# Entry of a one-core decoder trunk: norm weights loaded in two parts, x transposed ahead of the first products

## The reference

```
for l in range(DEPTH):
    xn = rms_norm(x, norm_mix_g[l])
    proj = xn @ w_in[l]                  # q, k, v and the inputs of three other mixers
    q = rope(q, positions); k = rope(k, positions)
    merged = sum of four mixers, each projected and gated by sigmoid(xn @ w_gate[l] + b_gate[l])
    x = x + merged @ w_o[l]
    hn = rms_norm(x, norm_ffn_g[l])
    gu = hn @ w_ffn_in[l]
    x = x + (silu(gu[..., :FF_DIM]) * gu[..., FF_DIM:]) @ w_ffn_out[l]
return rms_norm(x, final_norm_g)
```

## Time and profile before

| | before |
|---|---|
| device time, median of 3 runs | 831.18 us (830.91 to 831.44) |
| the profiled execution: its own time | 831.92 us |
| the profiled execution: its span | 830.2 us |
| TensorE busy | 817.8 us (99%) |
| VectorE busy | 612.2 us (74%) |
| ScalarE busy | 459.0 us (55%) |
| GpSimd busy | 153.6 us (18%) |
| DMA | 156.17 MB, mean 188 GB/s |
| mean granted TensorE clock | 0.994 of full speed |

### The profile page before, as it was taken

How to read it: one execution, slowest core, us unless ns; L and a number is a source line. 1 busy time by engine, 2 the same in 40 slices (tenths; PEclk the granted TensorE clock), 3 DMA queues, 4 the chain that set the end, 5 groups by cost and what they waited for, 6 DMA issues and landing times.

```text
span 830.2 us, 12730 instructions
## 1 busy us (share of the span) xinstructions
PE 817.8 (99%) x4963; PEld 721.3 (87%) x4963; DVE 612.2 (74%) x732; ACT 459.0 (55%) x625; POOL 153.6 (18%) x147
## 2 busy tenths in 40 slices
PE   7999999999999999999999999999999999999997
PEld 6999888888989999999999988888899888888885
DVE  3989788986786666656697798888687667666664
ACT  4847776634465545454565567765355545454544
POOL 6005756064000000000000285623300000000000
PEclk8999999999999999999999999999999999999999
DMA  9876555556545755564558655464645464655451
GB/s 277 274 217 197 196 165 178 185 196 219 188 139 163 238 183 174 199 205 161 195 170 254 199 179 165 167 231 159 204 157 198 152 199 159 221 181 192 162 178 51
DMA packets 103533, 156.17 MB, mean 188 GB/s; under 512 B 4016, under 2 KB 68834, under 8 KB 103488
## 3 DMA queue, kind: packets, MB, share of 16 engines
q1 hardware_dynamic: 100928, 152.45, 55.6%
q0 software_dynamic: 1328, 1.79, 0.7%
q10 hardware_dynamic: 1232, 1.31, 0.5%
HBM read 152.39 MB, written 1.05 MB: 185 GB/s over the span
## 4 chain that ended last, share of the span: by engine, by line
PE 93%; DVE 3%; ACT 1%; DMA 1%; issue 1%; POOL 0%; DVEq 0%; ACTq 0%; POOLq 0%
PE bank L1047 19%; PE bank L1049 10%; PE bank L992 8%; PE bank L994 8%; PE bank L993 8%; PE bank L935 7%; PE bank L936 7%; PE bank L937 7%; PE bank L1024 5%; PE bank L1023 5%; PE bank L1022 5%; DVE w_lo L1386 1%; DMA gain_rows<-in_norm_ffn_g 1%; ACT w_hi L625 1%; PE bank L1128 1%
## 5 line engine op out<-in xcount | busy, mean ns | idle before, releaser
L1386 DVE TENSOR_TENSOR w_lo<-raw,w_hi 128x2048 fp32r<-128x2048 f32 x136 | 320.7, 2360 | 133.7 <-ACT w_hi L625 133.1
L625 ACT ACTIVATE w_hi<-raw 128x2048 fp32r<-128x2048 f32 (+1 forms) x144 | 263.9, 1839 | 131.4 <-PE bank L994 55.8
L1047 PE MATMUL bank<-act,w_hi 128*128 128x512 f32 x704 | 247.6, 395 | 0.0
L1049 PE MATMUL bank<-act,w_lo 128*128 128x256 f32 x704 | 196.9, 280 | 0.0
L1047 PEld LDWEIGHTS bank<-act,w_hi 128*128 128x128 f32 x704 | 132.0, 188 | 30.3
L1049 PEld LDWEIGHTS bank<-act,w_lo 128*128 128x128 f32 x704 | 132.8, 189 | 0.4
L992 PE MATMUL bank<-w_hi,act 128*128 128x512 f32 x288 | 114.3, 397 | 0.0
L994 PE MATMUL bank<-w_hi,act 128*128 128x512 f32 x288 | 112.3, 390 | 0.0
L993 PE MATMUL bank<-w_lo,act 128*128 128x512 f32 x288 | 112.1, 389 | 0.0
L625 ACT ACTIVATE qk<-bank 128x256 f32<-128x256 f32 (+1 forms) x96 | 37.5, 394 | 76.4 <-PE bank L1049 76.3
L935 PE MATMUL bank<-act,w_hi 128*128 128x256 f32 x256 | 74.0, 289 | 0.4 <-DVE act L1409 0.2
(11 more groups left out here) (243 smaller groups left out, 1417.3 us busy)
## 6 DMA issues: line engine op xcount, KB each, us to landing
raw<-in_w_ffn_in SPq DMA_DIRECT2D x44, 1024.0 KB, 5.1
raw<-in_w_gate SPq DMA_DIRECT2D x32, 1024.0 KB, 5.5
raw<-in_w_ffn_out SPq DMA_DIRECT2D x22, 1024.0 KB, 4.9
raw<-in_w_in SPq DMA_DIRECT2D x20, 1024.0 KB, 5.8
raw<-in_w_o SPq DMA_DIRECT2D x8, 1024.0 KB, 5.0
raw<-in_w_proj_b SPq DMA_DIRECT2D x4, 1024.0 KB, 4.9
gates<-qk SPq DMA_DIRECT2D x32, 64.0 KB, 4.4
raw<-in_w_proj_a SPq DMA_DIRECT2D x2, 1024.0 KB, 4.9
```

What stands on the lines that cost most here:

```text
L625: return nc.scalar.activation(o, i, ACT.Copy)
L1047: nc.tensor.matmul(bank[b + f], hi[:, k, fs], act2[:, k, :, :].rearrange("p h s -> p (h s)"), start=(k == 0), stop=False, skip_group_check ...
L1049: last = nc.tensor.matmul(main(b)[:, f, :], lo[:, k, fs], act_hi[:, k, :], start=False, stop=(k == KT - 1), skip_group_check=True)
L1386: V.tensor_tensor(w_lo[slot][:, :], raw[slot][:, :], w_hi[slot][:, :].bitcast(F32), ALU.subtract)\
```

## The change

The norm weights of the mixers (`norm_mix_g`, 16 rows) are loaded by ACT's queue right behind x piece 0, and those of the feed-forward part (`norm_ffn_g`) by POOL's queue behind the parameter rows and `icnt`. They are turned and copied separately: the first at the entry, the second at unit 4 of layer 0 beside the parameter rows. ACT's queue now carries x piece 0, the weights, x piece 2, quarter 1; SP's carries quarter 3 as well, ahead of unit 1. PE runs 34 dummy products instead of 24, turns x piece 0 before the norm weights, then pieces 1 and 2, and runs 12 dummies; piece 3 is turned after quarter 0. On DVE `reduce_angles` moves from unit 1 to unit 2, behind `norm_scale`.

```diff
@@ sp
             load_x(sp, 3)
+            load_quarter(sp, 0, 3)
             for i in range(4):
                 load_quarter(sp, 1, i)
@@ gpsimd
             nc.gpsimd.memset(zeros[:, :], 0.0).then_inc(pre_const, 1)
-            for i, name in enumerate(("norm_mix_g", "norm_ffn_g")):
-                pool.dma_start(gain_rows[i * L * KT:(i + 1) * L * KT, :], T[name].rearrange("l (r p) -> (l r) p", p=P))\
-                    .then_inc(gain_in, 16)
             nc.gpsimd.memset(ident[:, :], 0.0).then_inc(pre_const, 1)
...
             pool.dma_start(icnt[:, :, :], inv_count).then_inc(icnt_in, 16)
+            pool.dma_start(gain_rows[FFN_GAINS:FFN_GAINS + L * KT, :], T["norm_ffn_g"].rearrange("l (r p) -> (l r) p", p=P))\
+                .then_inc(ffn_gain_in, 16)
@@ scalar
             load_x(act, 0)
+            act.dma_start(gain_rows[0:L * KT, :], T["norm_mix_g"].rearrange("l (r p) -> (l r) p", p=P))\
+                .then_inc(gain_in, 16)
+            load_x(act, 2)
             load_quarter(act, 0, 1)
-            load_x(act, 2)
-            load_quarter(act, 0, 3)
...
+                    if l == 0:
+                        copy(gains[:, L * KT:2 * L * KT], bank[6][:, P:P + L * KT])
                     copy(par[:, 0:r0], bank[6][:, 0:r0])
@@ tensor, at unit 4
+                    if l == 0:
+                        pe.wait_ge(ffn_gain_in, 16)
+                        fg = slice(FFN_GAINS, FFN_GAINS + L * KT)
+                        nc.tensor.transpose(bank[6][:, P:P + L * KT], gain_rows[fg, :], ident[fg, fg])
                     nc.tensor.transpose(bank[6][:, 0:N_ROWS], rows[:, :], ident[0:N_ROWS, 0:N_ROWS])\
@@ tensor, entry
             pe.wait_ge(pre_const, 1)
-            warm(24)
+            warm(34)
             pe.wait_ge(pre_const, 3)
-            pe.wait_ge(gain_in, 16 * 2)
-            nc.tensor.transpose(bank[0][:, 0:2 * L * KT], gain_rows[:, :], ident[0:2 * L * KT, 0:2 * L * KT])\
+            first_x(0)
+            pe.wait_ge(gain_in, 16)
+            nc.tensor.transpose(bank[0][:, 0:L * KT], gain_rows[0:L * KT, :], ident[0:L * KT, 0:L * KT])\
                 .then_inc(pre_pe, 1)
-            first_x(0)
-            warm(4)
             first_x(1)
-            warm(8)
+            first_x(2)
+            warm(12)
             pe.wait_ge(gains_ready, 1)
             for i in range(4):
-                if i in (1, 2):
-                    first_x(i + 1)
+                if i == 1:
+                    first_x(3)
                 pe.wait_ge(act_lo_ready, i + 1)
                 last = quarter(0, i)
@@ vector
             dve.wait_ge(pre_pe, 1)
-            V.tensor_copy(gains[:, :], bank[0][:, 0:2 * L * KT]).then_inc(gains_ready, 1)
+            V.tensor_copy(gains[:, 0:L * KT], bank[0][:, 0:L * KT]).then_inc(gains_ready, 1)
...
-                    if l == 0 and u == 1:
-                        reduce_angles()
                     if u == 1 + (l == 0):
                         norm_scale(l, 0)
+                    if l == 0 and u == 2:
+                        reduce_angles()
                     misc(l, u)
```

More of the change, by code:

```diff
@@ L114 @@
 N_ROWS = 70
+FFN_GAINS = 32
 DVE_CHAIN_PER_LAYER = 66
@@ L197, in build @@
         rows = sb("rows", [N_ROWS, P])
-        gain_rows = sb("gain_rows", [2 * L * KT, P])
+        gain_rows = sb("gain_rows", [FFN_GAINS + L * KT, P])
         gains = sb("gains", [P, 2 * L * KT])
@@ L309, in build @@
         gain_in = sem("gain_in")
+        ffn_gain_in = sem("ffn_gain_in")
         gains_ready = sem("gains_ready")
```

## The result

| | before | after |
|---|---|---|
| device time, median | 831.20 us (830.31 to 831.65, 20 runs) | 832.58 us (832.04 to 834.39, 20 runs) |
| ratio after / before | | 1.0019, interval 1.0012 to 1.0026 |
| the profiled execution: its own time, its span | 831.92, 830.2 us | 832.36, 830.6 us |
| first product of unit 0 | 12.04 | 8.78 |
| first product of unit 2 | 26.20 | 25.27 |

What follows compares the result with a forecast made beforehand. Two chains, from the norm weights through TensorE and from unit 2's landing, were taken to bound unit 2's start. Terms -0.9 (unit 2), -0.45 (norm), +0.1 (transpose) sum to -1.25, giving a median of 829.9 us, range 828.5 to 831.7.

Steps and rivals of the forecast that it cites:

- two chains that meet at unit 2: At unit 2's first product: one chain through TensorE from the norm weights, one from unit 2's landing, meeting at 26.20.
- landing 21.0: Unit 2's load: still lands at 21.0, with the same 5.36 MB ahead of its end; range 20.2 to 21.6.
- first product of unit 2 at 25.3: Unit 2: products start at 25.3 instead of 26.2, 0.9 us gained, as DVE starts the low part earlier.
- TensorE through unit 1 at 21.2: Units 0 and 1: TensorE is through at 21.2, or by about 24 if the clock is low at first.
- no wait left in front of the norm's product: Norm's product after unit 3: the 0.45 us wait goes, as DVE has the norm ready at about 34.7.
- the sum against the profiled execution: Whole kernel: -0.9 - 0.45 + 0.1 = -1.25, so 830.67 us for the profiled execution's own time.
- The clock: Rival at the wait before unit 2: the clock falls, costing 1.4 to 2.8 us, total 831.3 to 832.7; chance 0.15.
- The base of the sum: Whole kernel: the runs' median stands 0.74 us below the profiled time, at 831.18, so it becomes 829.9.
- The transpose: At unit 4: one more transpose on TensorE for the feed-forward weights, taken as 0.1 us, up to 0.28.
- The uneven engines: Unit 2's landing: some DMA engines ahead of others; rival of a landing at 20.2 gives 829.1 us, chance 0.22.
- it doesn't do what it says: Entry: norm weights land at 7.75 or beyond; time stays the forecast's, loss only beyond about 10; no separate chance.
- the whole entry gain: Rival at unit 2: it does not bind, needing a landing at 17; -5.0 - 0.45 + 0.1 gives 825.8 us; chance 0.04.

Runs made afterwards that it cites:

- after_again: The changed kernel run again unchanged as a control: 832.83 us, ratio 1.0017 to the kernel before; its profiled execution took 830.63 us.
- fill_wait: The changed kernel with 64 more dummy products between unit 1 and unit 2: 831.19 us, ratio 0.9995 to the kernel before.
- no_dummies: The changed kernel without its 34 and 12 dummy products: 831.42 us, ratio 0.9999 to the kernel before.
- before_filled: The kernel before with 90 dummies at its start instead of 24: 831.55 us, ratio 1.0006.
- late_spread: Changed kernel with POOL's loads held until unit 2 lands, matrices until unit 5 lands, one transpose at unit 4, dummies spread (40, 8, 8): 826.39 us.
- before_pool_late: The kernel before with POOL's loads behind the norm weights held until unit 2 has landed: 830.87 us, ratio 1.0000.

## Why the prediction was wrong

**What held.** The view of two chains that meet at unit 2, and each time on it: landing 21.0 (measured 20.88), first product of unit 2 at 25.3 (25.27), TensorE through unit 1 at 21.2 (21.1), a wait of 4.1 us (4.00), and no wait left in front of the norm's product. The 21.2 came true partly by luck. I had unit 0 start between 9.3 and 10.8 and its last quarter held to about 14 by ACT and DVE. It started at 8.78, below that range, and from 10.97 on the products follow each other without a wait; the last quarter began at 13.91 by TensorE's own pace. The execution of after_again without a fall took 830.63, and the sum against the profiled execution had said 830.67. That agreement is luck in part too: its unit 2 began 0.3 us earlier than forecast (24.98), and its transposes cost 0.2 us more.

**The clock (the step that failed).** The forecast put the fall of the clock in the new wait at nothing. I had the mechanism as a rival, with the right place and a price of 1.4 to 2.8 us, and gave it 0.15. The measured 832.58 lies inside that rival's 831.3 to 832.7. The range up to 831.7 took in only the lowest 0.4 of those 1.4 us, not the lower half as I wrote. In the two profiled executions the other terms came close: -0.93 for -0.9, -0.44 for -0.45, +0.31 for +0.1; the clock's +1.56 stands where the sum has no term. It is the normal case: one timing of 11 in after_again, and none of the 20 of after, lies below 831.9, and the fall in the others is inferred from that. The measured price is 1.5 us in the pair of traces and 1.6 between the medians of after_again and fill_wait. I had argued that the wait was about as long as the idle time after which the clock fell in the earlier trace rows, called that open, and then priced it as unlikely. A wait about as long as one that goes with a fall in a trace at hand speaks for it. no_dummies shows that even 2.3 us can do.

**The base of the sum.** I took the gain at unit 2, 0.9 us, from one profiled execution (26.20), and then moved the whole result down by the 0.74 us by which that execution lay above the median. I read these as the same 0.7 us. In the profiled execution TensorE came late to unit 2 after the low clock of the earlier trace rows; before_filled shows that without that loss the kernel before is held by the landing as well. If all behind unit 2's start is alike, the median of 831.2 belongs to a start at some 25.5 (26.20 less 0.7) and not at 26.2, and the change has little to gain there. It is an inference for the runs without a trace, and what held unit 2 in them is not shown. The numbers nearly close with no gain there at all: 831.2 - 0.44 (norm) + 0.31 (transpose) = 831.07 without a fall, and fill_wait measures 831.19; with 1.6 for the fall 832.7, and after measures 832.58.

**The transpose.** I took 0.1 for it from a gap of 0.03, with 0.28 as the upper end; it measured 0.31. One small transpose between products had cost next to nothing; a second one beside it did.

**The uneven engines.** I counted it as a chance for a gain. The landing varied between 20.2 and 21.6 in the traces with POOL's loads in place, so the range of 20.2 to 21.6 held, but it moves before and after alike and favours neither.

**Rival "it doesn't do what it says"** did not come: the norm weights were turned at 6.15.

**Rival "the whole entry gain"** did not come either, but I had written that nothing brings unit 2 in by 17. Holding POOL's loads does (17.88, and 16.14 to 16.54 in three other traces), and late_spread's 826.39 is near that rival's 825.8.

## What to carry to other kernels

Before an entry is made faster, follow the first transfer that it does not touch from its landing through every split to the products: if that chain ends where TensorE arrives now, an earlier arrival only becomes a wait, and a wait of a few us may cost TensorE's clock on top. Such a gain comes out once the other chain is shortened too, here by holding 1 MB of loads, of which TensorE reads the first at 45 us (3.6 us under the kernel before), or by cutting the unit into quarters (3.0 us). The hold brings nothing without the early entry; the quarters were not tried without it. A profiled execution that lies above the median must be asked what in it was slow before its waits are put down as a gain; the same loss must not be counted as a gain and as an offset. And a granted clock of 1.00 is checked against the rate of the rows before it is believed.

## What the runs showed of the hardware

At unit 2 the clock fell about 1 us after TensorE had begun to work again, not during the wait: in after the wait ended at 25.27 and the fall came at 26.3; in no_dummies it ended at 24.59 and the clock was 0.78 of full speed from 25 to 26 on average and 0.50 from 26 on. At the entry of before it fell during the wait, near 7.6. The length of the wait alone doesn't decide it: 2.31 us brought a fall, 2.92 us in after_again did not. The granted clock can also read 1.00 where TensorE works at half rate: in before_pool_late four transposes take 1.11 us at a reading of 1.00, and 1.12 in before at 0.50. The low clock was also not equally long with TensorE busy: in after it was over 3.4 us after the fall (29.7), while at the entry of the kernel before TensorE worked at it from 8.77 to 14.4. The Trainium skill, "TensorE: Matmul & The Clock Gate", section "Part 1: The HAM clock gate", warns that the same kernel meets the gate differently from run to run. The traces of after and after_again agree: the same kernel turned an x piece in 0.66 us at the entry of one and ran at half rate to 9.8 us in the other, and fell to 0.50 at unit 2 only in the first.
